# Moving 32 more prompt tokens of a product-key expert layer from dense products to gathered rows

## What is computed

```python
def peer(h, w_pq, sub_keys, u_tab, v_tab):          # 8 heads, 128 x 128 experts
    q = (x @ w_pq).reshape(T, 8, 2, 128)
    s = einsum('thpd,phnd->thpn', q, sub_keys)       # 16 score rows of 128 a token
    s1, i1 = top_k(s[:, :, 0], 16); s2, i2 = top_k(s[:, :, 1], 16)
    top, pos = top_k(s1[..., :, None] + s2[..., None, :], 16)
    eidx = take_along_axis(i1 * 128 + i2, pos)       # 16 experts a head, 128 a token
    gate = softmax(top)
    a = einsum('thkd,td->thk', u_tab[eidx], x)
    return einsum('thk,thkd->td', gelu(a) * gate, v_tab[eidx])
```

## Time and profile before

| | |
|---|---|
| median of 3 runs | 1716.5 us (1716.44 to 1719.83) |
| the profiled execution | 1716.78 us, span 1715.0 us |
| PE busy | 97% of the span, 10,559 matmuls |
| DVE, ACT, POOL busy | 69%, 39%, 66% |
| HBM | 407.64 MB read, 51.83 MB written, 268 GB/s over the span |

### The profile page before, as it was taken

The page is one execution under the profiler, slowest core; times in us unless marked ns, Lnnn a source line. Parts: engine busy times, 40 slices in busy tenths (PEclk is TensorE's granted clock), DMA queues, the critical chain, the costliest instruction groups (busy, mean ns, idle before and its releaser), DMA issues.

```text
span 1715.0 us, 27259 instructions
## 1 busy us (share of the span) xinstructions
PE 1666.8 (97%) x10559; PEld 1598.4 (93%) x10559; DVE 1182.1 (69%) x2276; ACT 665.1 (39%) x1055; POOL 1132.8 (66%) x677
## 2 busy tenths in 40 slices
PE   8999999899999999989999999999999999999996
PEld 3899878697999999989999999999999999999996
DVE  4340244645779689899888888446887877878745
ACT  2554222333334333333344334334444444444432
POOL 1767322132335889976766676778999798999952
PEclk9999999999999999999999999999999999999998
DMA  8645213044204889979999999979999999999951
GB/s 277 217 150 160 74 65 105 17 143 148 89 36 144 303 272 323 329 241 331 360 341 353 350 359 344 339 304 343 398 409 401 368 392 410 401 408 398 397 196 65
DMA packets 192706, 461.27 MB, mean 269 GB/s; under 512 B 21185, under 2 KB 99009, under 8 KB 192449
## 3 DMA queue, kind: packets, MB, share of 16 engines
q1 hardware_dynamic: 79872, 242.31, 40.0%
q0 software_dynamic: 46080, 167.79, 26.1%
q10 hardware_dynamic: 66624, 49.42, 8.7%
HBM read 407.64 MB, written 51.83 MB: 268 GB/s over the span
## 4 chain that ended last, share of the span: by engine, by line
PE 83%; DVE 9%; DMA 3%; POOL 3%; issue 2%; ACT 1%; SPq 0%; DVEq 0%; ACTq 0%; POOLq 0%
PE ps L929 51%; PE ps L699 18%; PE ps L940 5%; DMA tab<-in_tab 3%; PE ps L719 2%; POOL tLo L655 1%; PE ps L728 1%; DVE ug L1580 1%; PE ps L902 1%; POOL ug L665 1%; DVE ps L1590 1%; DMA raw<-in_w 1%; PE ps L834 1%; DVE eqb L1692 0%; PE ps L856 0%
## 5 line engine op out<-in xcount | busy, mean ns | idle before, releaser
L655 POOL TENSOR_TENSOR tLo<-tab,tHi 128x1024 fp32r<-128x1024 f32 x256 | 624.0, 2438 | 150.9 <-ACT tHi L1179 148.1
L1179 ACT CAST tHi<-tab 128x1024 fp32r<-128x1024 f32 x256 | 267.8, 1046 | 290.4 <-PE ps L929 210.0
L929 PE MATMUL ps<-hHi,tLo 128*128 128x384 f32 x1024 | 347.3, 339 | 4.1 <-POOL tLo L655 3.3
L929 PE MATMUL ps<-actHi,tLo 128*128 128x384 f32 x1024 | 342.8, 335 | 2.1 <-POOL tLo L655 1.4
L929 PE MATMUL ps<-hHi,tHi 128*128 128x384 f32 x1024 | 342.8, 335 | 0.0
L929 PE MATMUL ps<-hLo,tHi 128*128 128x384 f32 x1024 | 342.7, 335 | 0.0
L929 PE MATMUL ps<-actLo,tHi 128*128 128x384 f32 x1024 | 342.1, 334 | 0.0
L929 PE MATMUL ps<-actHi,tHi 128*128 128x384 f32 x1024 | 342.1, 334 | 0.0
L643 POOL TENSOR_TENSOR wLo<-raw,wHi 128x1024 fp32r<-128x1024 f32 x53 | 128.2, 2419 | 290.2 <-ACT wHi L1011 290.2
L1580 DVE SCALAR_TENSOR_TENSOR ug<-ug,ps 128x1024 f32<-128x1024 f32 x160 | 191.2, 1218 | 55.1 <-DMA ug<-in_urows,eidx 50.2
L1590 DVE SCALAR_TENSOR_TENSOR ps<-ug,act_s,ps 128x1024 f32<-128x1024 f32 x158 | 202.7, 1283 | 5.4 <-DVE ps L1590 0.5
(11 more groups left out here) (355 smaller groups left out, 2479.3 us busy)
## 6 DMA issues: line engine op xcount, KB each, us to landing
tab<-in_tab SPq DMA_DIRECT2D x256, 512.0 KB, 6.7
raw<-in_w SPq DMA_DIRECT2D x101, 512.0 KB, 4.2
gate_scratch<-stage ACTq DMA_DIRECT2D x48, 512.0 KB, 7.0
gt<-gate_scratch SPq DMA_DIRECT2D x32, 768.0 KB, 6.9
gelu_scratch<-ga ACTq DMA_DIRECT2D x112, 192.0 KB, 5.7
gin<-gelu_scratch SPq DMA_DIRECT2D x112, 192.0 KB, 9.2
ug<-in_urows,eidx POOLq DMA_INDIRECT x160, 7.0
ug<-in_vrows,eidx POOLq DMA_INDIRECT x160, 7.4
```

The lines of the kernel that those rows point to most:

```text
L655: pool.tensor_tensor(tLo[:, n % SPL], tab[:, n % TABS], tHi[:, n % SPL].bitcast(F32), ALU.subtract).then_inc(s_tlo, 1)
L929: last = mm(ps[:, bank, 0:TD], w, x[:, k, 0:TD], start=first, stop=end)
L1179: nc.scalar.copy(tHi[:, n % SPL], tab[:, n % TABS]).then_inc(s_thi, 1)
```

## The change

Of the 384 dense prompt tokens 32 become sparse. They join the 32 samples: 64 tokens in BG = 2 groups of 64 partitions, 64 picks of each token per group, so PB = 64 items; NDOT = 192, NIT = 384. TD = 352, so products have 352 columns, there are 11 gate blocks and NSTEP = 44 steps. The retrieval for the grouped tokens handles four heads per partition in place of two.

The constants of the order move: the first 64 items at chunks 8 to 55 (32 at 7 to 38 before), 72 dots in the retrieval (46), the swap at chunk 57 (39), transposes at 63 (50), gate steps at chunks 64 to 116, 2.5 dots a step (2), and 18 row additions per 11 chunks in the second half (10 per 7).

The product of the first one-hot with the gate goes from DVE to ACT: per step eight in-place passes of 128x128 with a per-partition scale, issued one step ahead and placed on ACT behind the gelu, cast and store of a chunk and ahead of the evacuations of the step. PE waits for them (s_wg) in place of DVE's one-hots. The gates' columns lie in SBUF now (gate_cols), not in PSUM; `oh1` goes.

```diff
-TD = T - P - TS
+NBT = 2 * TS
+BG = P // NBT
+TD = T - P - NBT
+TA = TD + P
+ARW = 384
-PB = P * TS // P
+PB = P // BG
-L2_DOTS = [0, 11, 22, 32, 46]
-N_SHUF = 50
-G_FIRST, G_SPAN = 51, 62
-N_SWAP = 39
+L2_DOTS = [0, 16, 32, 52, 72]
+N_SHUF = 63
+G_FIRST, G_SPAN = 64, 54
+N_SWAP = 57
-N_FOLD = NCH + 40
+N_FOLD = NCH + 44
+def dots_until(steps):
+    return L2_DOTS[-1] + 5 * steps // 2
 def sparse_until(n):
     if n < NCH:
-        return min(NDOT, L2_DOTS[-1] + 2 * NSTEP + 2 * (n - G_FIRST - G_SPAN))
-    return NDOT + max(0, min(NDOT, (n - N_GELU) * 10 // 7))
+        return min(NDOT, dots_until(NSTEP) + 2 * (n - G_FIRST - G_SPAN))
+    return NDOT + max(0, min(NDOT, (n - N_GELU) * 18 // 11))
 def item_time(q):
     if q < PB:
-        return 7 + q
+        return 8 + q * 48 // PB
     if q < early:
-        return N_SWAP + (q - PB) * 9 // (early - PB)
-    if q < early + 2 * NSTEP:
-        return G_FIRST + (q - early) // 2 * G_SPAN // NSTEP
+        return N_SWAP + (q - PB) * 6 // (early - PB)
+    if q < dots_until(NSTEP):
+        return G_FIRST + (q - early) * 2 // 5 * G_SPAN // NSTEP
...
-    return N_GELU + (q - NDOT) * 7 // 10
+    return N_GELU + (q - NDOT) * 11 // 18
...
-        oh1 = at("oh1", [P, STEP_TOK, P], pos_sq + 1024)
+        gate_cols = at("gate_cols", [P, TD], pos_sq + 1024)
...
             def gate_product(st):
-                pe.wait_ge(s_oh, st + 1)
+                pe.wait_ge(s_wg, st + 1)
...
+            def weight_one_hots(st):
+                act.wait_ge(s_oh, st + 1)
+                for t in range(STEP_TOK):
+                    q = STEP_TOK * st + t
+                    last = f(w1[:, st % 2, t, :], w1[:, st % 2, t, :], ACT.Identity, scale=gate_cols[:, q:q + 1])
+                last.then_inc(s_wg, 1)
...
+                if n == G_FIRST - 1:
+                    weight_one_hots(0)
                 for st in gate_steps(n):
                     b, j = st // 4, st % 4
+                    if st + 1 < NSTEP:
+                        weight_one_hots(st + 1)
...
             where = [best_b[:, 1], best_b[:, 2]]
-            retrieve(2, m16_b[:], ix_b[:], best_b[:, 0], where, lambda part: None)
+            retrieve(PH // BG, m16_b[:], ix_b[:], best_b[:, 0], where, lambda part: None)
...
-                if st:
-                    v.wait_ge(s_oh, st)
-                link(tt(oh1[:], keys_, over(idx12[:, 0, at_], P), ALU.is_equal))
-                tt(w1[:, st % 2], oh1[:], over(g_cols[:, at_], P), ALU.mult).then_inc(s_oh, 1)
+                tt(w1[:, st % 2], keys_, over(idx12[:, 0, at_], P), ALU.is_equal).then_inc(s_oh, 1)
             for st in range(NSTEP):
                 one_hots(st)
-                sparse(L2_DOTS[-1] + 2 * (st + 1))
+                sparse(dots_until(st + 1))
```

More of the change, by code:

```diff
@@ L283, in build @@
         ug = at("ug", [P, UG, D], SPL_AT)
[L284 to L288, removed]
+        ga = [at(f"ga{i}", [P, TD], (SPL_AT + 24576, SPL_AT + 24576 + 4 * TD, pos_sq + 6912)[i]) for i in range(3)]
+        idx12 = at("idx12", [P, 2, TD], SPL_AT + 27392)
+        a_s = at("a_s", [P, NDOT], SPL_AT + 30208)
+        act_s = at("act_s", [P, NDOT], SPL_AT + 30976)
+        eidx = at("eidx", [P, NDOT], SPL_AT + 31744, U32)
         peer_end = Z_AT + 59392
@@ L291, in build @@
         identR = at("identR", [P, P], cmask_at, F32R)
-        fold = at("fold", [P, TS], SPL_AT + 32640)
+        fold = at("fold", [P, NBT], SPL_AT + 32512)
         zp = [Z_AT]
@@ L975, in _ @@
                     for k in range(KT):
-                        last = mm(ps[:, late_bank(n + 2), k * TS:(k + 1) * TS], y_b[:, k * P:(k + 1) * P], fold[:],
+                        last = mm(ps[:, late_bank(n + 2), k * NBT:(k + 1) * NBT], y_b[:, k * P:(k + 1) * P], fold[:],
                                   start=True, stop=True)
@@ L1204, in _ @@
                 rows = pair(U_PQ + j)
[L1205 removed]
+                f(q_b[:, j % 2].rearrange("p (g t) -> p g t", g=BG), rows[:, TA:T].unsqueeze(1).broadcast_to([P, BG, NBT]),
                   ACT.Identity)
@@ L1218, in _ @@
             for i, x in enumerate((hHi, hLo)):
-                last = nc.scalar.copy(h_b[:, i].rearrange("p k (g t) -> p k g t", g=4),
-                                      x[:, :, TP:T].unsqueeze(2).broadcast_to([P, KT, 4, TS]))
+                last = nc.scalar.copy(h_b[:, i].rearrange("p k (g t) -> p k g t", g=BG),
+                                      x[:, :, TA:T].unsqueeze(2).broadcast_to([P, KT, BG, NBT]))
             last.then_inc(s_hb, 1)
@@ L1701, in indices @@
                 stt(out, where[0], float(NKEY), where[1], ALU.mult, ALU.add).then_inc(s_eidx, 1)
-            for g in range(P // TS):
-                nc.vector.tensor_copy(fold[TS * g:TS * (g + 1), :], ident[TS * g:TS * (g + 1), TS * g:TS * (g + 1)])
+            for g in range(BG):
+                nc.vector.tensor_copy(fold[NBT * g:NBT * (g + 1), :], ident[NBT * g:NBT * (g + 1), NBT * g:NBT * (g + 1)])
             link(nc.vector.tensor_copy(ranks[:], iota[:, 0:PK].unsqueeze(2).broadcast_to([P, PK, 2 * PH * PK])))
             where = [best_b[:, 1], best_b[:, 2]]
-            retrieve(2, m16_b[:], ix_b[:], best_b[:, 0], where, lambda part: None)
+            retrieve(PH // BG, m16_b[:], ix_b[:], best_b[:, 0], where, lambda part: None)
             indices(eidx[:, 0:PB], where)
```

57 lines of the change are left out of this document (29 added, 28 removed).

## The result

The kernel after takes **1733.16 us** (median of five runs, 1728.57 to 1736.53) against 1716.66 (1716.44 to 1719.83) beside it: a ratio of 1.0090, 95% interval 1.0073 to 1.0106. It is slower by 16.5 us. The profiled execution took 1729.33 us, its span 1727.6.

A forecast was written before the change was run, and what follows sets the result against it. It took POOL to bound chunks 9 to 63, the DMA engines the gate stage, and both the second half: 802 + 2.5 + 311 + 41.3 + 555 + 17.5 = 1729.5 us of span, 1731 us; own range 1716 to 1746, wider 1699 to 1757.

The forecast's parts named there:

- First indices: Retrieval before the first gather: four heads in place of two delay POOL and PE by 4.5 us, ends nothing and 9.
- Chunks 9 to 63 held by POOL: Before the gate stage: POOL needs 211.5 us plus 16 lost beside DVE's bfloat16 passes, 227.5; chunk 64 starts at 802.
- Gate stage held by the DMA engines: Chunks 64 to 117: 117.7 MB take 311 us, against 285 for PE; the first step adds 2.5 us.
- middle rate: Gate stage: 379 GB/s, taken between 355 and 403 because stores of small rows stay in the mix, giving 311 us.
- The clock of TensorE: Whole kernel: idle PE could lose its clock; priced at nothing because an earlier stretch with gaps kept 1.00.
- The first rival: DMA engines have room and the gate stage runs at PE's pace, 285 instead of 311 us: 1705 us total; chance 0.26.
- The second rival: DMA binds harder than POOL: gate stage 332 us at 355 GB/s, late tables in the second half, total 1761; chance 0.20.
- Chunks 118 to 127: Between gate stage and second half: 38.3 us at PE's pace plus 3 for SP standing at the first gate read-back.
- Second half: Chunk 128 on: POOL at 4.33 us a chunk and DMA at 4.32 bind together, 555 us, plus a 17.5 us tail.
- The sign that the prediction named: Chunks 9 to 63 and 129 to 245: PE's idle is ended by POOL's subtractions; second-half chunks average 4.3 to 4.4 us.
- the sign of being wrong: Second half: POOL waiting for ScalarE's casts would show the forecast wrong.
- PE: Table products: 352 columns cost 0.33 us less a chunk than 384, 84 us over 256 chunks if PE stays the bound.

The follow-up runs named there:

- e2: Kernel after with POOL subtracting only the first half of each table tile from chunk 4 on, all bytes kept: 1688.78 us.
- e6: Kernel after with DVE taking dots 62 and 63 before its long run of bfloat16 passes instead of after it: 1733.15 us.
- e1: Kernel after with every gather from the seventh item on taking half a row (256 KB instead of 512 KB), same number of gathers: 1712.53 us.
- e4: Kernel after with table products of 320 instead of 352 columns, except in the first chunks of each half: 1730.33 us.
- e3: Kernel after with both half-row gathers and half the subtraction on POOL: 1625.73 us.
- e7: Kernel after with the 112 gelu stores issued from SP, five tables behind their chunk, instead of from ScalarE's queue: 1746.49 us.
- e8: Kernel after with 14 first-half subtractions and every fourth of the second half moved from POOL to DVE, dots 62 and 63 early: 1754.83 us.
- e5: Kernel after with the gate weighting moved back from ScalarE to one DVE pass a step, both inputs in SBUF: 1764.07 us.

## Why the prediction was right

It said 1731 us, and the result is 1733; its sum for the span was 1729.5 (the terms as written add up to 1729.3), the profiled one 1727.6. Chunk 64 came 5.7 us late and the stages behind it 7.3 us short of their terms together, so an agreement within 2 us is in part luck. By its steps:

- **First indices.** Predicted 4.5 us of delay, the tenth subtraction at 565.2. Measured 564.17, 3.5 us later than in the earlier trace rows; 1.4 of them lie ahead of the retrieval (the first product started at 523.3 against 521.9), so the retrieval cost 2.1.
- **Chunks 9 to 63 held by POOL.** Right, shown by e2: with POOL relieved, PE is full. The loss beside DVE's bfloat16 passes, taken over as 16 us, measured 17.0: 76 gathers from 564 to 808 at a mean of 1.128 us in place of 0.95 are 13.5, 56 subtractions at 2.462 in place of 2.40 are 3.5. Still chunk 64 came at 807.7, not at 802. From the tenth subtraction to that of chunk 63 POOL took 232.8 us (564.17 to 796.92) in place of 227.5. The step that was too short is the one that let DVE follow POOL freely: dots 62 and 63 wait behind DVE's passes, so PE stood 7.3 us at the swap, POOL 3.4 for ScalarE's cast behind it, and the weighted picks came at 806.07, not at 800. e6 shows that taking the two dots earlier does not win the time back, so the swap is not the whole cause of the delay.
- **Gate stage held by the DMA engines.** Right, shown by e1 (bytes away: 293.2, PE full) against e2 and e4 (POOL or PE relieved: 308.4 and 309.5). The middle rate of 379 GB/s that I chose stands beside 378 measured over the stage, a closer hit than the argument for it deserves: between 355 and 403 nothing in the earlier trace rows singled it out, and the rate is no ceiling of the mix. Two stretches inside the stage show that:

```profile
850.00:900.00 50.00, 44.09 (x288) 43.51 (x288) 35.33 (x47) 32.67 (x84) 34.76 (x25) 0.93 1.01 370
900.00:950.00 50.00, 50.00 (x353) 50.00 (x352) 38.49 (x53) 37.39 (x90) 39.02 (x28) 1.00 1.04 388
```

  PE was full at 388 GB/s and lost time at 370, so the mean takes in spells in which the transfers came late and others in which they kept up. PE's pace there, 285 us by the sum, was 289.1 in e3. The weighting took 2.45 us a step, 2.2 predicted. That ScalarE's queue would be held by its own DMA issues was not foreseen; e7 shows that it adds nothing to the stage.
- **The clock of TensorE** was priced at nothing, and it was not nothing. Beside waits of PE the lower of its two levels (1.2 of 2.4 GHz) was granted for a while: 10.2 us at the swap, where PE stood from 771.8 to 779.1, and three times in the gate stage, 13.6 us together, beside waits of 2.7, 4.9 and 3.1 us. A wait of 2.9 us in the second half, at 1359.6, left it at the upper level. Two of these stretches, columns as in the earlier trace rows:

```profile
774.40:784.70 10.30, 5.59 (x23) 5.59 (x24) 6.50 (x8) 0.00 (x0) 9.54 (x6) 0.50 0.72 218
...
890.50:897.30 6.80, 5.22 (x22) 5.22 (x23) 1.40 (x2) 6.80 (x20) 2.81 (x2) 0.50 0.82 278
```

  In the gate stage PE was busy 294.6 of 309.5 us, in e3, at a granted clock of 1.00, 286.4 of 289.1 for the same products. So by an estimate from these numbers some 8 of the 20 us over e3 are the slower clock behind the waits and the rest more waiting; no run took the clock by itself.
- **The first rival**, gate stage at PE's pace, needed 413 GB/s. The best 50 us of the stage, 1000 to 1050, had 400. The Trainium skill's 425 GB/s for a large load (DMA: Bandwidth & Descriptors, section on measured bandwidth) is not reached in any of these mixes of small and large rows, its 358 for the HBM side (section on where 436 GB/s comes from) is passed in most of them: 378 with stores, 404 and 416 in second halves of loads.
- **The second rival**, 355 GB/s and late tables throughout, gave 1761 and fell with the rate; the range stated, up to 1757, did not reach it. In the second half the tables did come late, but ScalarE's wait was 53.0 us in 20 places, less than the 80.2 of before; with POOL relieved it grew (e2, e8), so here POOL sets the pace first.
- **Chunks 118 to 127** took 40.0 us, 41.3 predicted. SP did stand 14.8 us for the last gate store, but from 1117 to 1157 PE was busy 38.97 of 40 us, so of the 3 us allowed for it about 1 came.
- **Second half.** POOL at 4.33 us a chunk, DMA at 4.32: measured 508.0/117 = 4.34. That they hold together is what e1 (508.3), e2 (494.6) and e3 (455.1) show; one alone would have let e1 or e2 fall to 455. The sign that the prediction named, PE's idle time ended by subtractions, came only in part. PE's waits from 1160 to 1700:

```profile
PE ps L938 <- DVE xT L1804: 19.7, 29, 0.7
PE ps L938 <- POOL tLo L664: 18.4, 42, 2.9
```

  The other half was ended by DVE's flush of a finished product, each time within 0.7 us. POOL waited 11.6 us for ScalarE's casts there, less than the 28.9 before, so the sign of being wrong stayed away.
- **PE.** That 352 columns would cost less was no matter: e4 takes 32 more away and gains nothing.

## What to carry to other kernels

Before work is moved off the busiest engine, price the same work on each engine and queue that it moves to, chunk by chunk: here a gather costs POOL 1.23 us and the DMA engines 0.5 MB, and neither had much left where PE was full. Where two limits lie within a few per cent, taking away either shows only the other; take both away in one run before calling either the bound. Neither a DMA share of 1.0 nor the rate by itself says that the engines hold a stage: PE ran without a gap at a share of 1.02, at 355 GB/s and again at 409, and lost time in the gate stage at 1.03 and 378. What told it was the run with fewer bytes. And a pass that goes back to its old engine is not the old pass if its inputs have moved: in e5 it cost twice as much.

## What the hardware showed besides

With the DMA engines at 378 GB/s on the mean, loads and stores mixed, the instruction that issues a DMA can itself hold its engine's queue: on ScalarE 23 of 48 stores took 0.48 to 7.24 us to issue, where one takes 0.33 us otherwise, and everything behind it in that queue waits, though the engine has nothing to do. The trace puts such time down to "issue". And a VectorE pass can be stretched far beyond its size by a GpSimd instruction under way: 128x512 in bfloat16 took 0.42 us in the kernel after and 3.17 in e6, where only two dots had changed places; 128x1024 in float32 took 1.22 us on the mean with one input in PSUM (kernel before) and 2.49 with both in SBUF (e5).
